# A second mixture of experts that loads its rows from memory in slot order, with its hidden products in column halves

## The reference, cut to what matters

```python
def expert_step(acc, p):
    w1e, w3e, w2e, c = p
    h = jax.nn.silu(x2d @ w1e) * (x2d @ w3e)
    return acc + c[:, None] * (h @ w2e), None
...
out, _ = lax.scan(expert_step, jnp.zeros_like(x2d), (w1, w3, w2, combine.T))
```

## Time and profile before

| | us |
|---|---|
| median of 3 runs | 803.46 (800.9 to 805.8) |
| profiled execution, its own time | 801.88 |
| its span, from the first instruction to the last | 799.9 |
| second mixture, first product of item 1 to the last | 623.0 to 772.2 |
| TensorE busy in the span | 687.1 (86%) |
| VectorE, ScalarE, GpSimd busy | 301.1, 217.9, 30.4 |
| mean granted TensorE clock | 0.943 |

### The profile page before, as it was taken

The page is one execution under the profiler, slowest core; times in us unless marked ns, Lnnn a source line. Parts: engine busy times, 40 slices in busy tenths (PEclk is TensorE's granted clock), DMA queues, the critical chain, the costliest instruction groups (busy, mean ns, idle before and its releaser), DMA issues.

```text
span 799.9 us, 19043 instructions
## 1 busy us (share of the span) xinstructions
PE 687.1 (86%) x7553; PEld 439.2 (55%) x7554; DVE 301.1 (38%) x900; ACT 217.9 (27%) x564; POOL 30.4 (4%) x46
## 2 busy tenths in 40 slices
PE   5998889879989899895569999969977999998854
PEld 4886568545545455452158457746853555554431
DVE  0898731461212222120354106871154222222115
ACT  1650350331212212110331014564051222222130
POOL 0000000200000000000200001100020000000010
PEclk9999899989999999997679999999989999999996
DMA  9999124206799799997399100020009978919804
GB/s 293 364 392 374 16 106 159 105 1 254 276 404 362 264 395 351 359 344 285 127 390 387 56 0 1 1 106 0 1 1 346 398 287 298 358 35 350 311 25 148
DMA packets 86825, 174.55 MB, mean 218 GB/s; under 512 B 7784, under 2 KB 21969, under 8 KB 86785
## 3 DMA queue, kind: packets, MB, share of 16 engines
q1 hardware_dynamic: 72912, 157.36, 53.6%
q10 hardware_dynamic: 11601, 8.13, 3.3%
q0 software_dynamic: 2272, 8.52, 3.0%
HBM read 162.99 MB, written 11.01 MB: 218 GB/s over the span
## 4 chain that ended last, share of the span: by engine, by line
PE 61%; DMA 19%; DVE 8%; ACT 4%; issue 3%; ACTq 2%; POOL 2%; SPq 0%; POOLq 0%; DVEq 0%
DMA ring<-in_moe_w 16%; PE ps L684 15%; PE ps L705 7%; PE ps L507 6%; PE ps L603 4%; PE ps L575 4%; PE ps L586 4%; PE ps L794 3%; PE ps L813 3%; PE ps L656 2%; PE ps L667 2%; PE ps L741 2%; PE ps L540 1%; PE ps L525 1%; POOL xT L463 1%
## 5 line engine op out<-in xcount | busy, mean ns | idle before, releaser
L684 PE MATMUL ps<-ring,work 128*32 128x256 f32 x2816 | 172.1, 398 | 26.9 <-issue 13.8
L684 PEld LDWEIGHTS ps<-ring,work 128*32 128x32 f32 x2816 | 99.7, 115 | 92.2 <-issue 41.4
L903 ACT ACTIVATE work<-ps 128x256 f32<-128x256 f32 (+4 forms) x160 | 55.5, 363 | 222.8 <-PE ps L705 96.5
L1406 DVE TENSOR_TENSOR work<-work,ps 64x256 f32<-64x256 f32 x44 | 18.7, 424 | 219.2 <-ACT work L1003 219.2
L705 PE MATMUL ps<-ring,work 128*32 128x256 f32 x1408 | 90.0, 384 | 1.1 <-DMA ring<-in_moe_w 1.1
L1184 DVE SCALAR_TENSOR_TENSOR work<-work,wdw 128x272 f32<-128x272 f32 x150 | 65.1, 499 | 1.0
L656 PE MATMUL ps<-tok,work 128*32 128x256 f32 x928 | 63.7, 382 | 1.7 <-DVE work L1389 1.7
L507 PE MATMUL ps<-xT,ring 128*128 128x272 f32 x256 | 59.1, 393 | 0.3 <-DVE xT L1161 0.3
L705 PEld LDWEIGHTS ps<-ring,work 128*32 128x32 f32 x1408 | 38.8, 109 | 34.4 <-DVE work L1408 10.4
L507 PEld LDWEIGHTS ps<-xT,ring 128*128 128x128 f32 x256 | 48.5, 190 | 10.3 <-DVE xT L1161 0.4
L1003 ACT ACTIVATE work<-ps 64x256 f32<-64x256 f32 x44 | 16.5, 375 | 127.7 <-PE ps L684 127.7
(11 more groups left out here) (229 smaller groups left out, 733.7 us busy)
## 6 DMA issues: line engine op xcount, KB each, us to landing
ring<-in_moe_w SPq DMA_DIRECT2D x120, 1024.0 KB, 11.9
ring<-in_conv_w_pw SPq DMA_DIRECT2D x12, 1024.0 KB, 12.2
ybuf<-work ACTq DMA_DIRECT2D x44, 128.0 KB
ybuf<-const POOLq DMA_DIRECT2D x2, 2048.0 KB, 8.1
ring<-in_kv_w_k SPq DMA_DIRECT2D x4, 1024.0 KB, 9.0
ring<-in_kv_w_v SPq DMA_DIRECT2D x4, 1024.0 KB, 10.8
ring<-in_attn_w_q SPq DMA_DIRECT2D x4, 1024.0 KB, 11.6
ring<-in_attn_w_o SPq DMA_DIRECT2D x4, 1024.0 KB, 10.8
```

Source lines behind the costliest of these rows:

```text
L684: last = pe.matmul(ps[SLOTS * q:SLOTS * (q + 1), 0, 0:256], xTg[:, k, :], w[:, k, (q % 2) * 256:(q % 2 + 1) * 256], start=(k == 0), stop=( ...
L903: return act.activation(dst, src, ACT.Copy)
```

## The change

It touches the second mixture alone, apart from the names of some semaphores.

- A tensor `xsort` in memory (36 blocks of 32 rows) is filled once near the start. After the second routing GpSimd scatters each token's row to its two slots (`sort_rows`, four indirect transfers of 512 KB), ahead of its other work.
- Item 0 is gathered as before. The rows of later items are read from `xsort` by ScalarE's queue into two buffers (`loaded_rows`), three items ahead, and ScalarE copies each to `xg`. The gather and VectorE's `pick` are gone from the loop.
- The products with w1 and w3 run over 128 columns of each quarter, then over the other 128, into two banks. Silu, gate, transpose and copy are done for each half, and the products with w2 are taken in the order 0, 2, 1, 3.
- TensorE's item loop carries a branch hint.

```diff
+            pool.dma_start(xsort.rearrange("(a p) d -> p a d", p=P),
+                           const[:, 0:D].unsqueeze(1).broadcast_to([P, SORTED * SLOTS // P, D])).then_inc(sem("y_filled0"), 16)
+            def sort_rows():
+                pool.wait_ge(sem("y_filled0"), 32)
+                pool.wait_ge(sem("pos_ready"), 2)
+                pool.wait_ge(sem("tok_ready1"), 2 * TILES[1])
+                for j in range(TILES[1]):
+                    for c in range(2):
+                        pool.indirect_dma_start(
+                            out=xsort, out_offset=bass.IndirectOffsetOnAxis(ap=pos_i[:, 1, c * 3 + j:c * 3 + j + 1], axis=0),
+                            in_=tok[:, j, :], in_offset=None,
+                        ).then_inc(sem("xsort_ready"), 16)
...
+            def sorted_item(g, b, it):
...
+                def hidden(part):
+                    for k in range(NC_):
+                        if k % 4 == 0 and part == 0:
+                            for m in range(2):
+                                pe.wait_ge(*arrived(b + m, k // 4, it))
+                        for q in range(QUARTERS):
+                            at = (q % 2) * 256 + part * P
+                            last = pe.matmul(ps[SLOTS * q:SLOTS * (q + 1), HIDDEN_BANK[part], 0:P], xTg[:, k, :],
+                                             w[q // 2][:, k, at:at + P], start=(k == 0), stop=(k == NC_ - 1),
+                                             skip_group_check=True)
+                    return last
...
+                pe.wait_ge(sem("xT_ready1"), g + 1)
+                hidden(0).then_inc(sem("h_begun1"), 1)
+                hidden(1).then_inc(sem("h_ready1"), 1)
+                turn_hidden(0)
+                pe.wait_ge(sem("xg_here"), g + 1)
+                for m in range(2):
+                    last = pe.transpose(ps[:, 3, m * P:(m + 1) * P], xg[:, m * P:(m + 1) * P], ident)
+                last.then_inc(sem("xg_turned1"), 1)
+                pe.wait_ge(sem("hT_ready1"), g * 2 + 1)
+                pe.wait_ge(*arrived(b + 2, 0, it))
+                output(0, True, False)
+                turn_hidden(1)
+                pe.wait_ge(*arrived(b + 2, 1, it))
+                output(2, False, False)
+                pe.wait_ge(sem("hT_ready1"), g * 2 + 2)
+                output(1, False, False)
+                output(3, False, True).then_inc(sem("y_ready1"), 1)
...
-                        with pe.Fori(lo, hi) as g:
-                            item(l, g, b, it)
+                        if l == 0:
+                            with pe.Fori(lo, hi) as g:
+                                item(l, g, b, it)
+                        else:
+                            with nc.Fori(lo, hi, engines=bass.OrderedEngineSet([pe.engine]), hint_back_edge=True) as g:
+                                sorted_item(g, b, it)
...
+                act.wait_ge(sem("xsort_ready"), 16 * 2 * TILES[1])
+                act.dma_start(loaded_rows[1], xsort[SLOTS:2 * SLOTS, :].rearrange("s (q c) -> q s c", q=QUARTERS)).then_inc(sem("xg_loaded1"), 16)
+                load(2, 0)
+                def item(g, buf, turn):
+                    act.wait_ge(sem(f"xg_loaded{1 - buf}"), turn * 16 + 16)
+                    act.wait_ge(sem("xg_turned1"), g + 1)
+                    move(xg, loaded_rows[1 - buf]).then_inc(sem("xg_here"), 1)
+                    act.wait_ge(sem("h_begun1"), g + 1)
+                    act.activation(hs[64:128, 0:P], ps[0:64, HIDDEN_BANK[0], 0:P], ACT.Silu).then_inc(sem("silu_ready1"), 1)
+                    act.wait_ge(sem("h_ready1"), g + 2)
+                    act.activation(hs[64:128, P:2 * P], ps[0:64, HIDDEN_BANK[1], 0:P], ACT.Silu).then_inc(sem("silu_ready1"), 1)
+                    act.wait_ge(sem("xg_here"), g + 1)
+                    load(g + 3, 1 - buf)
+                    act.wait_ge(sem("y_ready1"), g + 2)
+                    act.wait_ge(sem(f"y_stored1_{buf}"), turn * 16 + 16)
+                    move(ysb[:, buf, :], ps[:, 1, 0:256]).then_inc(sem("y_moved1"), 1)
+                    act.wait_ge(sem("y_moved1"), g + 1)
+                    act.dma_start(ybuf[1][bass.ds(g * SLOTS, SLOTS), :].rearrange("s (q c) -> q s c", q=QUARTERS),
+                                  ysb[:, buf, :]).then_inc(sem(f"y_stored1_{buf}"), 16)
...
+                with dve.Fori(0, n) as g:
+                    gate(g, 0)
+                    move_hidden(g, 0)
+                    gate(g, 1)
+                    move_gathered(1, g + 1, True)
+                    move_hidden(g, 1)
```

More of the change, by code:

```diff
@@ L53 @@
 MIN_ITEMS = 2 * SEQ // SLOTS
+SORTED = MAX_ITEMS + 4
 TILES = [(T0 + P - 1) // P, SEQ // P]
@@ L163, in trunk @@
         ybuf = [nc.dram_tensor(f"ybuf{l}", (MAX_ITEMS * SLOTS, D), F32, kind="Internal").ap() for l in range(2)]
+        xsort = nc.dram_tensor("xsort", (SORTED * SLOTS, D), F32, kind="Internal").ap()
         def cst(name):
@@ L182, in scores_of @@
             return ps[:, 2:4, 0:KEYS[1]]
+        HIDDEN_BANK = (0, 5)
+        loaded_rows = view(512, 256), view(1152, 256)
         def m_bank(c):
@@ L466, in _ @@
                 scale(l)
+                if l == 1:
+                    sort_rows()
                 pool.wait_ge(sem("tab_ready"), l + 1)
@@ L634, in post_norm_and_route @@
                                                 stream[l][:, 4 * q + c, j * P:j * P + rows], ident)
-                        last.then_inc(sem(f"tok_turned{l}"), 1)
+                        last.then_inc(sem("tok_turned"), 1)
                 pe.wait_ge(sem("picks_ready"), l + 1)
@@ L707, in item, with turn_hidden, output @@
                 last.then_inc(sem(f"y_ready{l}"), 1)
+            def sorted_item(g, b, it):
+                w = [brick(b + m).rearrange("p (k n) -> p k n", k=NC_) for m in range(2)]
+                w2 = brick(b + 2).rearrange("p (k n) -> p k n", k=4)
+                def hidden(part):
[9 more added lines that the diff above has]
+                    return last
+                def turn_hidden(part):
+                    pe.wait_ge(sem("hs_ready1"), g * 2 + (part + 1))
+                    pe.sem_inc(sem("turn_begun"), 1)
+                    pe.transpose(ps[:, 4, part * 64:(part + 1) * 64], hs[64:128, part * P:(part + 1) * P],
+                                 ident[64:128, 64:128]).then_inc(sem("h_turned1"), 1)
+                def output(k, first, final):
+                    for q in range(QUARTERS):
+                        last = pe.matmul(ps[SLOTS * q:SLOTS * (q + 1), 1, 0:256], hT[:, k, :], w2[:, k, q * 256:(q + 1) * 256],
+                                         start=first, stop=final, skip_group_check=True)
+                    return last
+                pe.wait_ge(sem("xT_ready1"), g + 1)
[15 more added lines that the diff above has]
+                output(3, False, True).then_inc(sem("y_ready1"), 1)
@@ L983, in post @@
                     for half in range(2):
-                        act.wait_ge(sem(f"tok_turned{l}"), 2 * j + half + 1)
+                        act.wait_ge(sem("tok_turned"), 6 * l + 2 * j + half + 1)
                         move(tok[0:rows_, j, half * 512:(half + 1) * 512], ps[0:rows_, 2 * j + half, :]).then_inc(sem(f"tok_ready{l}"), 1)
@@ L989, in post, with sorted_items, load @@
                 act.activation(e2[:, 0:n], e2[:, 0:n], ACT.Exp).then_inc(sem("e2_ready"), 1)
+            def sorted_items(n):
+                def load(g, odd):
+                    act.dma_start(loaded_rows[odd],
+                                  xsort[bass.ds(g * SLOTS, SLOTS), :].rearrange("s (q c) -> q s c", q=QUARTERS)).then_inc(sem(f"xg_loaded{odd}"), 16)
+                act.wait_ge(sem("xsort_ready"), 16 * 2 * TILES[1])
[17 more added lines that the diff above has]
+                                  ysb[:, buf, :]).then_inc(sem(f"y_stored1_{buf}"), 16)
+                with act.Fori(0, n >> 1) as turn:
+                    item(turn * 2, 0, turn)
+                    item(turn * 2 + 1, 1, turn)
+                with act.If(n & 1):
+                    item(n - 1, 0, n >> 1)
+                act.wait_ge(sem("xg_loaded0"), (n >> 1) * 16 + 16)
+                act.wait_ge(sem("xg_loaded1"), ((n + 1) >> 1) * 16 + 16)
+                combine(1, 0)
             def mixture(l):
@@ L998, in mixture @@
                     act.sem_inc(sem(f"y_stored{l}_{buf}"), 16)
+                if l == 1:
+                    return sorted_items(n)
                 def item(g, buf, turn):
@@ L1032, in combine @@
                     rows_ = min(P, TOKENS[l] - j * P)
[L1033 to L1034 removed]
+                    act.wait_ge(sem("stats_ready"), 3 * l + j + 1)
+                    act.activation(tstd[0:rows_, j:j + 1], mv[0:rows_, j, 1:2], ACT.Sqrt, bias=cst("eps")[0:rows_, :]).then_inc(sem("tstd_ready"), 1)
                     if l == 0:
@@ L1386, in pick_item @@
                                             pos2[:, c, 0:n].unsqueeze(2).broadcast_to([P, n, SLOTS]), ALU.is_equal)
+                if l == 1:
+                    step(ins)
```

(15 more changed lines are left out.)

6 lines of the change are left out of this document (2 added, 4 removed).

## The result

The changed kernel takes 841.62 us (median of 4 runs, 838.54 to 842.07), the kernel before, run beside it, 802.18 us (4 runs, 799.99 to 805.8). The ratio is 1.048, with a 95% interval of 1.043 to 1.053: slower by 39 us. I had forecast 809, range 793 to 824. The direction was right, the size was not.

The account below looks back on a forecast made before the run. The start was taken as bound by transfers, the items by TensorE and its waits inside an item. From the profiled 801.9 us, plus 7.5 for the start, minus 2.1 for the items: 807.3, or 809 on the median's scale; range 793 to 824.

Parts of the forecast that it names:

- Part 1: Second mixture's items: with the gather gone and silu and gate in halves, an item with nothing late on ScalarE takes 6.25 us.
- Part 2: Products with w1 and w3 in half width: 3.5 us an item as now, weight loads hidden; upper bound 0.86 us more.
- the rival with exposed weight loads: Half-width products: weight loads show, 0.86 us in each of 11 items without table loads, 818 us in all; chance 0.10.
- Part 3: ScalarE's loop body: two table loads in each turn's first item delay silu, that item takes 8.1 us, TensorE stands nearly 2.
- Part 4: Items 1 to 20 of the second mixture: 141.7 us against 143.8 before, a gain of 2.1 us; loop entries stay.
- The clock rival: Even items of the second mixture: the clock falls behind holes of nearly 2 us, nine falls of 1.7 us, 824; chance 0.10.
- Part 5: Start of the second mixture: waiting for scatters and the first row load makes item 1 start 7.5 us late, at 630.5.
- Part 6: Priced at nothing: the sorted tensor's fill, row loads and DMA issues in odd items' slack, renamed semaphores, the branch hint.
- Code fetch: TensorE's longer item loop: each of 14 back edges stalls for an instruction fetch, 30 us, 839 in all; chance 0.04.

Follow-up runs that it names:

- the run with the hint alone: The kernel before with the branch hint on TensorE's item loop of the second mixture and nothing else: 804.76 us, ratio 1.006.
- the second longer-code run: The kernel before with a block of 48 products, always jumped over, behind each item of the second mixture: 814.7 us, ratio 1.016.
- the run with the transfers alone: The kernel before with the sorted tensor, its fill and four scatters added but read by nobody, items still gathered by TensorE: 808.02 us, ratio 1.007.
- the run with fewer weights in flight: The changed kernel with ScalarE's copy behind the first silu and two halves of bricks in flight instead of four: 819.33 us, ratio 1.021.

## Why the prediction failed

- **Part 1, the odd item: right.** 6.25 forecast, 6.28 measured.
- **Part 2, half-width products: right.** 3.5 us, and the rival with exposed weight loads did not come. The prediction counts records as products in places (the 64 in 3.46 us are 32 products of two records each); its price per record is not touched by that.
- **Part 3, two table loads: right.** The trace has 10 and 10, silu of an even item at 4.9 (forecast 5.0), the item 8.27 to 8.56 (forecast 8.1), TensorE's hole 2 us.
- **Part 4, the items' sum: wrong.** 141.7 with 3.7 for entries and 1.7 for the clock is 147.1; measured 171.4. Of the 24.3 more, 8.05 are the two stops (4.99 and 3.06). TensorE was busy for 143.6 us where 20 items of 6.28 are 125.6, 18.0 more. By item that is 5.7 in items 7 to 9, behind the stops; 8.2 behind the holes of even items; 3.2 at the two entries of the outer loop, where I had 1.7; and 0.9 spread over items at full clock. So the first pass through the longer code, which my sum had at nothing, cost 13.8 us with the clock behind it, and the falls behind even items' holes, also at nothing, 8.2.
- **The clock rival: right in price, right in total only by luck.** I had written it down as nine falls of 1.7 us, 15 us, with a chance of 0.10. Five came, at 1.6 each. That the whole loss to the clock is 16.3 us above my 1.7, near those 15, is an accident: nearly half of it stands behind stops and entries. I had read a rule out of two rows, 2.16 us with a fall and 1.51 without. The runs don't bear it out. Items 6, 10 and 14 have the same hole of 1.95 us as item 12 and keep the clock; and where the entry of 2.16 us had a fall behind it, one of 2.28 us in the run with the hint alone and one of 2.55 us in the second longer-code run had none (3.66 us for the products, not 5.35).
- **Part 5, the start: a term mis-sized.** Item 1 starts at 640.65, not 630.5. The step that failed is the load of one item's rows: it was put at 3 us, from stores that ran with memory idle, and took 10.23, beside the weights and with a second load on the same queue. The scatters land at 622.29 (forecast 620), 2.3 more. The rest of the chain was within 0.7 us. I gave 4 and 10 us as bounds; it was 17.6. That the weights, pushed to 627.4, would not be far ahead or behind is borne out: in the run with the transfers alone they let item 1 begin at 629.8.
- **Part 6, at nothing: the hint wrong, the fill right.** The fill is hidden: in the run with the transfers alone the weights are first issued at 601.7 us, before at 601.6. The hint does not stand at the entry of a loop: the trace has it 21 times, once an item. It comes with 1.4 us of stop even in the short body.
- **Code fetch, the rival with 0.04:** right that longer code costs, wrong place. No back edge of an item waits; what waits is the first pass through a later expert's code. The Trainium skill, "Runtime: NRT & Kernel Launch", on instruction fetch, speaks of a taken branch outside the resident window; the stops here are in straight code behind such an entry, and the jump over the block in the longer-code run, taken in every item, cost nothing.
- **What the sum would have been.** 807.3, 10.1 for the start and 24.3 for the items are 841.7; the profiled execution took 842.07. These terms come from its own trace, so they say where the time went; what causes it is for the experiments.
- **Behind these, mostly hidden until the table load was moved:** ScalarE's queue did not carry a load and a store per item. In the changed kernel as it stands even items are slow enough that this showed mostly at the start.

Left open: why some holes of 2 us let the clock fall and some do not; whether the stops are waits for code (item 8 has none in the run with fewer weights in flight), and which fetch the hint displaces in item 7. Not tried: rows in fewer, larger packets, and a filler of products in the even items' hole.

## What to carry to other kernels

Count what a queue must carry per item, not only bytes over the whole: 264 packets of 1 KB per 6.4 us were too many beside the weights, though the DMA engines' mean share was 0.66. If a longer lead doesn't help, suspect that the queue is full; give the loads a queue of their own. And before a loop body that is unrolled several times is made longer, look at the first pass through each copy: its price is paid once per copy, with the clock behind it.

## What the runs showed of the hardware, unexpected

- A queue with 1 KB packets beside a saturating stream of weights got some 26 packets per us, with two queues 38 to 43 together; one load of 128 KB landed after 8 to 17 us, where 3.31 us had been its like in quiet memory.
- A block of 192 instructions that is always jumped over cost 12.8 us between the medians: no time per item, a stop of 3.11 us with lower clock behind it, and 14.68 us of standing ahead of the code behind the loop, where the kernel before has 9.28.
- 96 records of one-column products, with full weight loads, took 15.7 to 18.6 us an item, 0.16 to 0.19 us each, at a mean granted clock of 0.70.
